# Second half's mixer paced over 331 instead of 277 expert loads, seams tile by tile, first loads ahead of head 1

## The chip, the cores and the metric

The kernel runs on one core of one Trainium2 chip. The metric is the device time of one execution in microseconds: 2576.68 as the median of three runs (2569.09 to 2582.97).

## The reference

512 tokens of width 1024 in float32 pass two blocks. The first: `x = x + concat(deltanet(h), pool(h)) @ w_out` with `h = rmsnorm(x)`, where the mixer is a chunked gated delta rule over 4 heads (short convolution, silu, normed q and k, the inverse of a triangular matrix by chunk, a state carried from chunk to chunk) beside a multi-scale pooling; then an expert layer:

```
q = (xb @ w_query).reshape(t, 8, 2, 128);  scores = einsum("thpc,hpkc->thpk", q, sub_keys)
s1, i1 = top_k(scores[:, :, 0], 16);  s2, i2 = top_k(scores[:, :, 1], 16)
top_s, top_pos = top_k((s1[..., :, None] + s2[..., None, :]).reshape(t, 8, 256), 16)
u = expert_down[idx];  v = expert_up[idx];  act = gelu(einsum("td,thkd->thk", xb, u))
x = x + einsum("thk,thkd->td", softmax(top_s) * act, v)
```

and a final norm. So each token reads 8 x 16 rows of `expert_down` and as many of `expert_up`, 537 MB in all. The second block: `x = x + gate_m * rmsnorm(attention(modulate(rmsnorm(x))))` with a stick-breaking attention of 16 heads, then the same frame around a SwiGLU FFN of inner width 2816. Shifts, scales and gates come from `silu(c) @ ada_w + ada_b`.

## The kernel before

Tokens lie as four tiles (T = 4) of 128. Each engine has its own program; semaphores order them. There are three parts.

**Front.** The first mixer and the query scores run in two halves (h = 0, 1) of 256 tokens. `front_plan(h)` writes the work of a half as a list of stages: `n0`, `tr0` norm and transposes; `p` 0 to 11 projections with convolutions `cv`; `ui`, `gr`, `mk`, `kt`, `ka`, `at`, `kk`, `aa` prepare a chunk of 128; levels 1 to 6 of `v`, `w`, `r`, `u` build the inverse of a chunk; `s1` to `s3` update the state; `pz`, `pl`, `pm` pooling and gate; `wo` output projection; `n1`, `tr1` the norm before the experts; `q` 0 to 15 query units, each followed by its scores `sc`; `gp`, `gs` the gates of the second block. Every engine walks through the same list and does its own share of each stage.

**Loads.** `paced` turns the list into load numbers: each stage's third value, `after`, is the number of expert loads (gathers) that pass before it. All up to the first half's q 6 stands at -1, ahead of the first load; q 7 stands at load 2, and the last stage (`gs` 3) at load 277. A load n is: GpSimd gathers 128 rows of 8 KB (`load`, L1508 to 1518) into a ring of RING = 8 buffers; VectorE multiplies with the tile's tokens and sums (L1816); ScalarE takes the gelu (`weigh`, L1306) and scales a diagonal (L1310); TensorE adds the pair of loads n - 1, n into two banks (`sums`), which frees two ring buffers. 16 loads make one head of one tile, 128 a tile, 512 in all. At a tile's end (loads 124 to 127 and so on) `spread_rows` and `fill_rows` spread the next tile's tokens and `evacuate` writes the tile's sum to x. A head's selection (`select`, `decode`, `spread_head`, `permute`, `place`) runs on VectorE, GpSimd, TensorE two heads ahead. On GpSimd the whole of the -1 part, with the selections of heads 0 and 1 (`sel` 0, `sel` 1), precedes the first eight loads. `Pace.upto(n)` runs the stages due by load n, behind load n's own work in each engine's loop. SP issues weight units (0.52 MB each, eight buffers, three for query units) in the order of the stages, each when the unit before it in its buffer is used, and between them pairs of modulation weights for loads 6 to 123.

Positions (first to last load of a group of stages) before: q 7 to q 15 of the first half 2 to 18; `n0`, `tr0` 19 to 22; `p` 25 to 57; preparation of chunk 2 65 to 77; its levels 77 to 101; state 101 to 107; preparation of chunk 3 108 to 120; its levels 120 to 144; state and pooling 144 to 167; `wo` 172 to 186; `n1`, `tr1` 189 to 192; q 0 to q 15 193 to 224; gates 228 to 277.

**Second block.** After load 511: `act_stats`, `rstd` norm all four tiles (final norm of block one, then the first norm of block two), `pe_transposes` (L670) transposes x, `evac_y` (L1355) modulates into y_hT, and VectorE's `split_hT` splits it in a high and a low part (L1842, L1844) for products of three matmuls each. Weights are split likewise (`split` on ScalarE, GpSimd L1538). GpSimd also fills the zeros of qz (L1543, L1544) behind the second unit. Behind the attention, `branch` takes the norm of the four sums at once and adds (L1882, L1883), then the same norm, transposes and splitting again, the FFN, and `branch` and one store of 2 MB.

## Time and profile before

| | us |
|---|---|
| median of three runs | 2576.68 (2569.09 to 2582.97) |
| profiled execution, its own time | 2573.54 |
| its span | 2571.7 |
| TensorE matmul busy | 1975.4 (77%) |
| VectorE busy | 1311.2 (51%) |
| ScalarE busy | 859.8 (33%) |
| GpSimd busy | 959.4 (37%) |
| first expert load issued, last landed | 255.6, 1801.3 |
| gathers' share of 16 DMA engines | 51.7% of the span |

The span is what the instructions cover; the execution's own time lies 1.8 us above. Busy shares are averages over stages with different limits, so the table by stretch is the one to read: a stretch there runs from the start of one load's dot product to that of another (loads 2, 18, 25, 58; 77, 101; 120, 144; 193, 228, 256; 278, 384, 392 in order of the rows). GB/s is what the DMA moved. In the timeline a row is one instruction or a merged run of like ones; the bracket is the idle time ahead of it and what ended it.

### The profile page before, as it was taken

The page shows a single profiled execution, that of the slowest core. Times are in us where ns is not written, and L with a number is a line of the kernel's source. Part 1 is how long each engine was busy: PE and PEld are TensorE (multiplying, and loading weights), DVE is VectorE, ACT ScalarE, POOL GpSimd, SP SyncE. Part 2 cuts the span into 40 slices and gives each one's busy share as a digit, 9 for nine tenths or more (in the row PEclk, how much of TensorE's full clock was granted, in tenths as well). Part 3 has the DMA queues.
Part 4 walks back from the last instruction along what each step waited for, and adds up shares of the span by engine and source line. Part 5 has one row for each costly group of instructions (what it writes and reads, how often), then busy time and mean ns, then how long its engine had stood idle before and what let it go on. Part 6 is the DMA issues. An engine that isn't in the chain of part 4 may idle for free.

```text
span 2571.7 us, 24837 instructions
## 1 busy us (share of the span) xinstructions
PE 1975.4 (77%) x8704; PEld 1153.5 (45%) x8704; DVE 1311.2 (51%) x2810; ACT 859.8 (33%) x2260; POOL 959.4 (37%) x725
## 2 busy tenths in 40 slices
PE   8897778878788868765556565555698996999996
PEld 7765555435334235311001110000487665888785
DVE  4523547677775554565667666765401542333301
ACT  3112233334343333333333333332423653222212
POOL 1200323356553333444454445544342002444342
PEclk9999888879799889888776787877799998999998
DMA  6112979989989899999999999999021001222221
GB/s 240 36 58 74 405 290 361 383 330 411 392 334 386 331 373 355 375 417 419 420 420 418 420 379 420 420 420 403 33 99 66 1 1 66 98 92 92 78 99 49
DMA packets 100668, 672.54 MB, mean 262 GB/s; under 512 B 11328, under 2 KB 11328, under 8 KB 31552
## 3 DMA queue, kind: packets, MB, share of 16 engines
q0 software_dynamic: 73728, 536.90, 51.7%
q1 hardware_dynamic: 26816, 134.06, 13.6%
q8 instruction: 69, 1.13, 0.2%
q14 instruction: 55, 0.45, 0.0%
HBM read 668.82 MB, written 2.10 MB: 261 GB/s over the span
## 4 chain that ended last, share of the span: by engine, by line
PE 56%; DMA 19%; DVE 8%; issue 6%; ACT 6%; POOL 5%; SPq 0%; DVEq 0%; POOLq 0%; ACTq 0%; PEldq 0%
PE ps L695 55%; DMA arena<-in_experts,arena_u 16%; POOL arena L1515 4%; DVE arena L1816 3%; DMA gtrow<-in_w_ada 1%; ACT arena L1310 1%; DMA arena<-in_w_ada 1%; ACT sel L1306 1%; ACT L1163 1%; PE ps L706 0%; DMA arena<-in_prow 0%; ACT arena L1169 0%; ACT arena L660 0%; ACT L1306 0%; DVE arena L1882 0%
## 5 line engine op out<-in xcount | busy, mean ns | idle before, releaser
L695 PE MATMUL ps<-arena 128*32 128x512 f32 (+4 forms) x4376 | 1125.3, 553 | 377.1 <-ACT arena L1310 362.7
L695 PEld LDWEIGHTS ps<-arena 128*128 128x128 f32 (+1 forms) x4376 | 493.1, 163 | 949.4 <-ACT arena L1310 539.8
L1515 POOL DMA_INDIRECT arena<-in_experts,arena_u x512 | 599.4, 1171 | 846.7 <-PE ps L695 757.5
L1816 DVE CUSTOM_DVE_ANT_0 arena<-arena 128x1024 f32<-128x1024 f32 x512 | 649.3, 1273 | 386.2 <-DMA arena<-in_experts,arena_u 374.6
L695 PE MATMUL ps<-r_low 128*128 128x512 f32 x1824 | 419.5, 392 | 9.7 <-DVE r_low L1844 7.6
L1538 POOL TENSOR_TENSOR r_low<-middle,r_low 128x1024 fp32r<-128x1024 f32 x98 | 235.6, 2404 | 512.7 <-ACT r_low L1349 512.7
L695 PEld LDWEIGHTS ps<-r_low 128*128 128x128 f32 x1824 | 343.3, 189 | 85.3 <-DVE r_low L1844 6.8
L1306 ACT ACTIVATE sel<-sel 128x1 f32<-128x1 f32 x512 | 102.3, 200 | 648.1 <-DVE sel L1816 647.2
L1349 ACT ACTIVATE r_low<-middle 128x1024 fp32r<-128x1024 f32 x98 | 103.6, 1058 | 281.4 <-PE ps L695 281.3
L1310 ACT ACTIVATE arena<-arena,sel 128x32 f32<-128x32 f32 x512 | 164.5, 321 | 17.2 <-ACT sel L1306 0.5
L695 PE MATMUL ps<-arena,consts 128*32 128x32 f32 (+2 forms) x544 | 75.0, 446 | 96.5 <-POOL arena L1498 69.4
L695 PE MATMUL ps<-r_low,r_high 128*128 128x512 f32 x528 | 122.4, 395 | 4.6 <-DVE r_high L1896 4.6
L1299 ACT ACTIVATE arena<-consts,arena 128x32 f32<-128x32 f32 x512 | 120.5, 306 | 0.0
L695 PEld LDWEIGHTS ps<-r_low,r_high 128*128 128x128 f32 x528 | 100.8, 191 | 26.2 <-DVE r_high L1896 5.0
L1894 DVE TENSOR_TENSOR middle<-middle,ps 128x512 f32<-128x512 f32 x22 | 15.1, 688 | 152.6 <-ACT middle L1432 152.6
L695 PEld LDWEIGHTS ps<-arena,consts 128*32 128x32 f32 (+1 forms) x544 | 20.1, 123 | 159.4 <-POOL arena L1498 93.3
L1879 DVE RECIPROCAL stat<-stat 128x4 f32<-128x4 f32 x2 | 0.4, 178 | 176.5 <-ACT stat L1422 176.5
L1491 POOL TENSOR_TENSOR sel<-sel 128x512 f32<-128x512 f32 x32 | 41.8, 1305 | 125.6 <-DVE sel L1614 125.0
L695 PEld LDWEIGHTS ps<-ccol,gtrow 128*128 128x128 f32 x512 | 68.5, 215 | 31.4 <-issue 31.2
L695 PE MATMUL ps<-ccol,gtrow 128*128 128x1 f32 x512 | 70.1, 267 | 7.8 <-DMA gtrow<-in_w_ada 7.8
L1273 ACT ACTIVATE arena<-ps 128x256 f32<-128x256 f32 x32 | 12.3, 384 | 146.8 <-PE ps L695 146.8
L1896 DVE TENSOR_TENSOR r_high<-middle,r_high 128x512 fp32r<-128x512 f32 x22 | 60.8, 2766 | 0.8
(201 smaller groups left out, 1518.9 us busy)
## 6 DMA issues: line engine op xcount, KB each, us to landing
middle<-in_w_late SPq DMA_DIRECT2D x24, 2048.0 KB, 7.4
arena<-in_w_front SPq DMA_DIRECT2D x88, 512.0 KB, 7.7
gtrow<-in_w_ada SPq DMA_DIRECT2D x32, 512.0 KB, 8.3
arena<-in_experts,arena_u POOLq DMA_INDIRECT x512, 12.1
arena<-in_w_ada SPq DMA_DIRECT2D x16, 512.0 KB, 9.0
x<-in_x SPq DMA_DIRECT2D x4, 512.0 KB, 9.0
arena<-in_sub_keys SPq DMA_DIRECT2D x2, 1024.0 KB, 10.4
arena<-in_rows SPq DMA_DIRECT2D x4, 512.0 KB, 10.3
```

The source lines that it names most:

```text
L695: return nc.tensor.matmul(out_, lhsT, rhs, start=start, stop=stop_, skip_group_check=skip)
L1163: nc.scalar.activation(sexp, tops, ACT.Exp, bias=nmax, accum_out=ssum).then_inc(s["sexp"], 1)
L1299: nc.scalar.activation(gated[:, m % 2, 32 * j:32 * j + 32], fold, ACT.Copy, scale=gq[:, i % 4, 4 * q + j:4 * q + j + 1]).then_inc(s["gated ...
L1306: own.step(nc.scalar.activation(gel[:, n % 8:n % 8 + 1], dots[:, n % 8:n % 8 + 1], ACT.Gelu))
L1310: nc.scalar.activation(diag[:, m % 4, 32 * j:32 * j + 32], gated[:, m % 2, 32 * j:32 * j + 32], ACT.Copy, scale=gel[:, n % 8:n % 8 + 1]).t ...
L1349: nc.scalar.activation(u_hi[u % 2], raw_unit(u), ACT.Copy).then_inc(s["u_hi"], 1)
L1491: tt(onehot, onehot, fidx.rearrange("p s (o a) -> p s o a", o=1).broadcast_to([P, 2, 16, 16]), ALU.mult).then_inc(s["fpk"], 1)
L1515: nc.gpsimd.indirect_dma_start(ring[n % RING], None, a["experts"], bass.IndirectOffsetOnAxis(ap=idxq[:, i % 4, k:k + 1], axis=0),).then_in ...
L1538: nc.gpsimd.tensor_tensor(u_lo[u % 2], raw_unit(u), u_hi[u % 2], ALU.subtract).then_inc(s["u_lo"], 1)
L1816: nc.vector.tensor_tensor_reduce(r[:, 0:D], r[:, 0:D], xrep[k % 4], 1.0, 0.0, ALU.mult, ALU.add, dots[:, n % 8:n % 8 + 1]).then_inc(s["dot ...
L1894: own.step(tt(ff[:, j % 2, :], ff[:, j % 2, :], ps[:, 2 * j % 8 + 1, :], ALU.mult))
L1896: tt(act_lo[:, j, :], ff[:, j % 2, :], act_hi[:, j, :], ALU.subtract).then_inc(s["ffd"], 1)
```

## The change

Pace: the second half's projections of odd number take 3 loads instead of 2, its inversion levels 5 instead of 4, its query units 2 to 15 take 4 instead of 2, the first half's query units 8 to 15 take 3 instead of 2. By the same list the positions are then: first half's q 7 to q 15 2 to 26; `n0`, `tr0` 27 to 30; `p` 33 to 71; levels of chunk 2 91 to 121, of chunk 3 140 to 170; `wo` 198 to 212; q 0 to q 15 219 to 278; gates 282 to 331.

First loads: on GpSimd the eight first gathers are issued right behind `sel` 0.

Seams: the norms of tiles 0, 1, 2 are done among the loads, at loads 337, 353, 433 (`beside`; two sums of squares on ScalarE 0 and 4 loads on, scaling and a diagonal matrix of the reciprocal root on VectorE 3 and 7 on, products with that diagonal on TensorE and the modulation on ScalarE 8 on), tile 3 behind the last load. Transposes are now products x with the diagonal. High parts of the activations move from VectorE to ScalarE. At the other two seams the norm goes tile by tile, and the store is four stores of 512 KB.

```diff
@@ -96,7 +96,7 @@
-        add("p", u, 2 if u else 3)
+        add("p", u, 3 if u == 0 or h == 1 and u % 2 == 1 else 2)
...
@@ -154,7 +154,7 @@
-                add("u", (c, lv), 2)
+                add("u", (c, lv), 2 + h)
...
@@ -215,7 +215,7 @@
-        add("q", j, 2)
+        add("q", j, 4 if h == 1 else 3 if j > 7 else 2)
...
@@ -461,6 +461,11 @@
+        def beside(n, lag):
+            gates = STAGES[-1][0]
+            return {gates + 6 + lag: 0, gates + 22 + lag: 1, gates + 102 + lag: 2}.get(n)
...
@@ -510,11 +515,11 @@
-        junk = region(130, D)
+        junk = region(140, D)
+        tdiag = region3(160, T, P)
-        xs2 = region3(144, T, D)
...
@@ -646,35 +651,18 @@
-            sp.wait_ge(s["fin"], T)
-            sp.dma_start(out.rearrange("b (t p) d -> p (b t) d", p=P), x[:, :, :]).then_inc(s["out"], 16)
-            sp.wait_ge(s["out"], 16)
-        def act_stats(eng, k, ready, junk_of):
-                ready(t)
-                if T * k + t > 0:
-                    eng.wait_ge(s["ssq"], T * k + t)
-                nc.scalar.activation(junk_of(t), x[:, t, :], ACT.Square,
-                                     accum_out=stat[:, 0, t:t + 1]).then_inc(s["ssq"], 1)
-            eng.wait_ge(s["ssq"], T * (k + 1))
-            nc.scalar.activation(stat[:, 1, :], stat[:, 0, :], ACT.Sqrt, bias=EPS, scale=1.0 / D).then_inc(s["sd"], 1)
-        def pe_transposes(eng, k, src):
-            for t in range(T):
-                eng.wait_ge(s["xs"], T * k + t + 1)
-                for kd in range(KD):
-                    ins = nc.tensor.transpose(ps[:, kd, t * P:(t + 1) * P], src[:, t, kd * P:(kd + 1) * P], ident)
-                ins.then_inc(s["tr"], 1)
+                sp.wait_ge(s["fin"], t + 1)
+                sp.dma_start(out.rearrange("b (t p) d -> p (b t) d", p=P)[:, t, :], x[:, t, :]).then_inc(s["out"], 16)
+            sp.wait_ge(s["out"], 16 * T)
-        tail_sq = region(8, D)
+        tail_sq, tail_sq2 = region(8, D), region(12, D)
...
@@ -1005,6 +993,17 @@
+            def tile_transposes(t):
+                pe.wait_ge(s["xs"], t + 1)
+                if t == 0:
+                    pe.wait_ge(s["gates_out"], N_GATE)
+                else:
+                    pe.wait_ge(s["a_y"], KD * t)
+                for kd in range(KD):
+                    ins = mm(ps[:, 1 + kd // 4, kd % 4 * P:(kd % 4 + 1) * P], x[:, t, kd * P:(kd + 1) * P], tdiag[:, t, :])
+                ins.then_inc(s["tr"], 1)
...
@@ -1310,6 +1316,27 @@
+            def tile_stats(t, n):
+                if n == 0:
+                    sc.wait_ge(s["acc_out"], t + 1)
+                else:
+                    sc.wait_ge(s["seln"], t + 1)
+                if t + n > 0:
+                    sc.wait_ge(s["ssq"], 2 * t + n)
+                if t == 0 and n == 0:
+                    sc.wait_ge(s["xrep"], 24)
+                nc.scalar.activation(junk, x[:, t, :], ACT.Square, accum_out=stat[:, 0, t:t + 1]).then_inc(s["ssq"], 1)
+                sc.wait_ge(s["ssq"], 2 * t + n + 1)
+                nc.scalar.activation(stat[:, 1, t:t + 1], stat[:, 0, t:t + 1], ACT.Sqrt, bias=EPS, scale=1.0 / D).then_inc(s["sd"], 1)
+            def tile_modulate(t):
+                sc.wait_ge(s["tr"], t + 1)
+                for kd in range(KD):
+                    nc.scalar.activation(y_hT[:, kd, t * P:(t + 1) * P], ps[:, 1 + kd // 4, kd % 4 * P:(kd % 4 + 1) * P], ACT.Identity,
+                                         bias=modc[:, 0, kd:kd + 1], scale=stat_mod(0, kd)).then_inc(s["a_y"], 1)
...
@@ -1330,13 +1357,16 @@
+                if beside(n, 0) is not None:
+                    tile_stats(beside(n, 0), 0)
+                if beside(n, 4) is not None:
+                    tile_stats(beside(n, 4), 1)
+                if beside(n, 8) is not None:
+                    tile_modulate(beside(n, 8))
-            sc.wait_ge(s["acc_out"], T)
-            act_stats(sc, 0, lambda t: None, lambda t: junk)
-            act_stats(sc, 1, lambda t: sc.wait_ge(s["seln"], t + 1), lambda t: junk)
+            tile_stats(T - 1, 0)
...
@@ -1348,16 +1378,18 @@
-            def evac_y(k):
-                sc.wait_ge(s["tr"], T * (k + 1))
-                for kd in range(KD):
-                    nc.scalar.activation(y_hT[:, kd, :], ps[:, kd, :], ACT.Identity, bias=modc[:, 2 * k, kd:kd + 1],
-                                         scale=stat_mod(k, kd)).then_inc(s["a_y"], 1)
+            def high(k, kd):
+                sc.wait_ge(s["a_y"], KD * T + kd + 1 if k == 1 else KD * T)
+                nc.scalar.activation(a_hi[:, kd, :], y_hT[:, kd, :], ACT.Copy).then_inc(s["a_hi"], 1)
+            sc.wait_ge(s["slot_done"], LOADS)
+            tile_stats(T - 1, 1)
-            evac_y(0)
+            tile_modulate(T - 1)
+            for kd in range(KD):
+                high(0, kd)
...
@@ -1410,20 +1442,33 @@
-            def branch(k):
-                for t in range(T):
-                    sc.wait_ge(s["y"], T * k + t + 1)
-                    if k + t > 0:
-                        sc.wait_ge(s["ysq"], (T + 1) * k + t)
-                    nc.scalar.activation(tail_sq, ps[:, 2 * t:2 * t + 2, :].rearrange("p b n -> p (b n)"), ACT.Square,
-                                         accum_out=stat[:, 2, t:t + 1]).then_inc(s["ysq"], 1)
-                sc.wait_ge(s["ysq"], (T + 1) * k + T)
-                nc.scalar.activation(stat[:, 3, :], stat[:, 2, :], ACT.Sqrt, bias=EPS, scale=1.0 / D).then_inc(s["ysq"], 1)
-            branch(0)
-            act_stats(sc, 2, lambda t: sc.wait_ge(s["yfree"], t + 1), lambda t: tail_sq)
-            evac_y(1)
+            def branch(k, t):
+                sc.wait_ge(s["y"], T * k + t + 1)
+                if k + t > 0:
+                    sc.wait_ge(s["ysq"], 2 * (T * k + t))
+                nc.scalar.activation(tail_sq, ps[:, 2 * t:2 * t + 2, :].rearrange("p b n -> p (b n)"), ACT.Square,
+                                     accum_out=stat[:, 2, t:t + 1]).then_inc(s["ysq"], 1)
+                sc.wait_ge(s["ysq"], 2 * (T * k + t) + 1)
+                nc.scalar.activation(stat[:, 3, t:t + 1], stat[:, 2, t:t + 1], ACT.Sqrt, bias=EPS, scale=1.0 / D).then_inc(s["ysq"], 1)
+            def stats_after(t):
+                sc.wait_ge(s["yfree"], t + 1)
+                sc.wait_ge(s["ssq"], 2 * T + t)
+                nc.scalar.activation(tail_sq2, x[:, t, :], ACT.Square, accum_out=stat[:, 0, t:t + 1]).then_inc(s["ssq"], 1)
+                sc.wait_ge(s["ssq"], 2 * T + t + 1)
+                nc.scalar.activation(stat[:, 1, t:t + 1], stat[:, 0, t:t + 1], ACT.Sqrt, bias=EPS, scale=1.0 / D).then_inc(s["sd"], 1)
+            for t in range(T + 1):
+                if t < T:
+                    branch(0, t)
+                if t >= 1:
+                    stats_after(t - 1)
+            sc.wait_ge(s["tr"], 2 * T)
+            for kd in range(KD):
+                nc.scalar.activation(y_hT[:, kd, :], ps[:, kd, :], ACT.Identity, bias=modc[:, 2, kd:kd + 1],
+                                     scale=stat_mod(1, kd)).then_inc(s["a_y"], 1)
+                high(1, kd)
...
@@ -1502,9 +1548,9 @@
-            front = Pace(front_program())
-            front.upto(-1)
+                    if stage == "sel" and arg == 0:
+                        for n in range(RING):
+                            load(n)
...
@@ -1517,8 +1563,9 @@
-            for n in range(RING):
-                load(n)
+            front = Pace(front_program())
+            front.upto(-1)
...
@@ -1805,6 +1852,18 @@
+            def tile_norm(t, n):
+                ve.wait_ge(s["sd"], 2 * t + n + 1)
+                own.step(nc.vector.reciprocal(stat[:, 1, t:t + 1], stat[:, 1, t:t + 1]))
+                if n == 0:
+                    ve.wait_ge(s["pfin"], 16)
+                    ve.wait_ge(s["acc_out"], t + 1)
+                    stt(x[:, t, :], x[:, t, :], stat[:, 1, t:t + 1], prow_fin, ALU.mult, ALU.mult).then_inc(s["seln"], 1)
+                else:
+                    ts(tdiag[:, t, :], ident, stat[:, 1, t:t + 1], None, ALU.mult).then_inc(s["xs"], 1)
...
@@ -1824,22 +1883,17 @@
-            rstd(0)
-            ve.wait_ge(s["acc_out"], T)
-            ve.wait_ge(s["pfin"], 16)
-            for t in range(T):
-                stt(x[:, t, :], x[:, t, :], stat[:, 1, t:t + 1], prow_fin, ALU.mult, ALU.mult).then_inc(s["seln"], 1)
-            rstd(1)
-            ve.wait_ge(s["seln"], T)
-            for t in range(T):
-                ts(xs2[:, t, :], x[:, t, :], stat[:, 1, t:t + 1], None, ALU.mult).then_inc(s["xs"], 1)
+                    if beside(n, 3) is not None:
+                        tile_norm(beside(n, 3), 0)
+                    if beside(n, 7) is not None:
+                        tile_norm(beside(n, 7), 1)
+            tile_norm(T - 1, 0)
+            tile_norm(T - 1, 1)
-                    ve.wait_ge(s["a_y"], KD * k + kd + 1)
-                    nc.vector.tensor_copy(a_hi[:, kd, :], y_hT[:, kd, :]).then_inc(s["a_hi"], 1)
...
@@ -1874,28 +1928,31 @@
-            def branch(k):
-                ve.wait_ge(s["ysq"], (T + 1) * (k + 1))
-                own.step(nc.vector.reciprocal(stat[:, 3, :], stat[:, 3, :]))
-                for t in range(T):
-                    y = ps[:, 2 * t:2 * t + 2, :].rearrange("p b n -> p (b n)")
-                    own.step(stt(tail[:, t % 2, :], y, stat[:, 3, t:t + 1], gtrow[:, k, :], ALU.mult, ALU.mult))
-                    tt(x[:, t, :], x[:, t, :], tail[:, t % 2, :], ALU.add).then_inc(s["yfree" if k == 0 else "fin"], 1)
-            ve.wait_ge(s["y"], T)
-            branch(0)
-            rstd(2)
-            ve.wait_ge(s["yfree"], T)
-            for t in range(T):
-                ts(xs2[:, t, :], x[:, t, :], stat[:, 1, t:t + 1], None, ALU.mult).then_inc(s["xs"], 1)
+            def branch(k, t):
+                ve.wait_ge(s["ysq"], 2 * (T * k + t + 1))
+                own.step(nc.vector.reciprocal(stat[:, 3, t:t + 1], stat[:, 3, t:t + 1]))
+                y = ps[:, 2 * t:2 * t + 2, :].rearrange("p b n -> p (b n)")
+                own.step(stt(tail[:, t % 2, :], y, stat[:, 3, t:t + 1], gtrow[:, k, :], ALU.mult, ALU.mult))
+                tt(x[:, t, :], x[:, t, :], tail[:, t % 2, :], ALU.add).then_inc(s["yfree" if k == 0 else "fin"], 1)
+            def norm_after(t):
+                ve.wait_ge(s["sd"], 2 * T + t + 1)
+                own.step(nc.vector.reciprocal(stat[:, 1, t:t + 1], stat[:, 1, t:t + 1]))
+                ts(tdiag[:, t, :], ident, stat[:, 1, t:t + 1], None, ALU.mult).then_inc(s["xs"], 1)
+            for t in range(T + 1):
+                if t < T:
+                    branch(0, t)
+                if t >= 1:
+                    norm_after(t - 1)
-            ve.wait_ge(s["y"], 2 * T)
-            branch(1)
+            for t in range(T):
+                branch(1, t)
...
```

## Rows read from the trace of the kernel before

**Rows 1.** The page: DMA share in tenths, 40 equal slices of the span.
```profile
DMA  6112979989989899999999999999021001222221
```

**Rows 2.** Busy time by stretch: us, PE, PEld, DVE, ACT, POOL busy (x instructions), clock, DMA share, GB/s.
```profile
267.30:318.60 51.30, 44.38 (x232) 30.91 (x228) 27.27 (x68) 15.52 (x54) 15.01 (x13) 0.97 1.01 410
318.60:367.00 48.40, 33.05 (x148) 20.50 (x150) 16.88 (x47) 16.68 (x52) 9.81 (x11) 0.78 0.77 289
367.00:483.10 116.10, 107.25 (x531) 68.34 (x528) 85.58 (x230) 41.17 (x131) 41.68 (x37) 0.87 0.91 355
554.90:623.50 68.60, 54.72 (x332) 31.07 (x328) 55.06 (x120) 23.86 (x88) 47.85 (x36) 0.93 1.00 409
681.60:754.80 73.20, 64.54 (x356) 32.40 (x356) 50.93 (x106) 31.02 (x96) 37.63 (x30) 0.87 0.84 322
929.00:1044.50 115.50, 95.97 (x430) 59.67 (x432) 60.63 (x157) 36.97 (x132) 37.58 (x33) 0.96 0.91 343
1044.50:1134.70 90.20, 61.76 (x250) 19.09 (x246) 50.68 (x119) 31.16 (x105) 39.58 (x36) 0.87 1.00 405
1201.60:1478.70 277.10, 150.75 (x490) 26.21 (x492) 184.94 (x448) 98.98 (x343) 133.58 (x118) 0.74 1.01 419
1478.70:1500.20 21.50, 14.42 (x86) 3.89 (x84) 16.08 (x49) 10.36 (x36) 9.26 (x9) 0.98 0.83 308
```

**Rows 3.** Timeline, 239 to 263: start, us, engine, line, operation, count, [idle before <-releaser].
```profile
240.07 0.17 DVE L1631 COPY arena<-ps 128x16 f32<-128x16 f32 x1
...
252.54 1.26 POOL L1491 TENSOR_TENSOR sel<-sel 128x512 f32<-128x512 f32 x1 [16.25 <-DVE sel L1614]
...
255.61 1.11 POOL L1515 DMA_INDIRECT arena<-in_experts,arena_u  x1 [0.17 <-issue]
...
255.92 0.17 DVE L1631 COPY arena<-ps 128x16 f32<-128x16 f32 x1
...
257.02 0.94 POOL L1515 DMA_INDIRECT arena<-in_experts,arena_u  x1 [0.30 <-issue]
...
261.40 1.23 DVE L1816 CUSTOM_DVE_ANT_0 arena<-arena 128x1024 f32<-128x1024 f32 x1 [5.31 <-DMA arena<-in_experts,arena_u]
```

**Rows 4.** Timeline, 1798 to 1843, from the last gathers to the attention block.
```profile
1798.22 1.91 PE L695 MATMUL ps<-arena 128*32 128x512 f32 x8 [1.59 <-ACT arena L1310]
...
1803.19 3.54 PE L695 MATMUL ps<-arena 128*32 128x512 f32 x8 [3.06 <-ACT arena L1310]
...
1812.55 1.28 ACT L663 ACT_TABLE_LOAD   x1
1813.84 0.20 ACT L663 ACTIVATE stat<-stat 128x4 f32<-128x4 f32 x1
...
1829.09 5.47 ACT L1355 ACTIVATE upper<-ps,modc 128x512 f32<-128x512 f32 x8 [6.47 <-PE ps L670]
...
1841.78 0.69 DVE L1844 TENSOR_TENSOR r_low<-upper,r_low 128x512 fp32r<-128x512 f32 x1
```

**Rows 5.** Timeline, 2155 to 2190, from the attention block to the FFN.
```profile
2155.82 1.01 ACT L1419 ACTIVATE arena<-ps 128x1024 f32<-128x1024 f32 x1
...
2174.84 5.50 PE L670 MATMUL ps<-consts,arena 128*128 128x128 f32 x32 [20.02 <-DVE arena L1890]
...
2189.09 0.69 DVE L1844 TENSOR_TENSOR r_low<-upper,r_low 128x512 fp32r<-128x512 f32 x1
```

**Rows 6.** Timeline, 2547 to 2572, the end.
```profile
2547.71 1.03 ACT L1419 ACTIVATE arena<-ps 128x1024 f32<-128x1024 f32 x1 [5.74 <-PE ps L695]
...
2554.83 1.28 DVE L1882 SCALAR_TENSOR_TENSOR arena<-ps,stat,gtrow 128x1024 f32<-128x1024 f32 x1
2556.15 1.23 DVE L1883 TENSOR_TENSOR x<-x,arena 128x1024 f32<-128x1024 f32 x1
...
2564.77 0.40 SPq L650 DMA_DIRECT2D out_dram<-x  x1
```

**Rows 7.** DMA issues: tile, queue, kind, count, KB each, median us to landing.
```profile
middle<-in_w_late SPq DMA_DIRECT2D x1, 1024.0 KB, 5.0
```

16 lines of the change are left out of this document (12 added, 4 removed).

## The prediction

> **What bounds the kernel now.** The page's slices come first [rows 1]: one slice is 64.3 us, and the 16 DMA engines stand at 8 or 9 tenths in nearly every one from 257 to 1801 us. In that stretch the 512 gathers of expert rows run, beside the mixer of the second half of the tokens. A gather is 128 rows of 8 KB, 1.05 MB; at the 419 GB/s of the stretch with nothing else in it, 1201.6 to 1478.7 [rows 2], that is 2.50 us each. The second view is the table by stage [rows 2]. Where its rate is near 419, the gathers set the time, and compute beside them is free; where it is lower, compute or a chain of waits sets it, and the lost time is length x (1 - rate/420). So: 1.2 us lost in the first half's last query units (267 to 319), 18.0 in the second half's projections (367 to 483), 1.8 in the inversion of chunk 2 (555 to 624), 17.1 in chunk 3's (682 to 755), 21.2 in the second half's query units (929 to 1044), 5.7 at the tile switch at load 384 (1479 to 1500). The third view is the timeline at four seams where TensorE stands still: the first gathers [rows 3], the hand-over from gathers to the attention block [rows 4], the hand-over to the FFN [rows 5] and the end [rows 6].
>
> **Pacing, 54 more loads.** By the list of stages the last stage moves from load 277 to 331: 8 loads more at the first half's query units 8 to 15, 6 at the projections, 6 + 6 at the levels of chunks 2 and 3, 28 at the second half's query units. No work goes; 54 of the loads that ran alone now run beside compute. A load taken out of the plain stretch saves 2.50 us there, and costs 2.50 where the DMA is already full, nothing but its own sum on TensorE where it isn't (a pair of sums 1.91 or 3.54 us [rows 4], 0.95 to 1.77 a load).
> Query units of the second half: 16 units in 115.5 us, 7.2 a unit with its two loads, of which TensorE is busy 96.0/16 = 6.0 and waits 1.2 [rows 2]. The DMA needs two gathers and a 0.52 MB unit, 5.00 + 1.25 = 6.25. With four loads: DMA 11.25, TensorE 6.0 + 1.9 + 2 x 1.2 = 10.3. The DMA becomes the bound and the 21.2 us go but for about 3: -18.
> Projections: 6 more loads at 1.4 us for the sum (between 0.95 and 1.77, as the clock there is 0.87) where 2.50 is saved: -6 of the 18.0.
> Inversion of chunk 2: only 1.8 lost before: -1. Chunk 3: its levels move from loads 120 to 144 to loads 140 to 170, so the tile switch at loads 124 to 128 falls out of them. A switch alone costs 5.7 and a chunk's inversion alone 1.8, so 17.1 - 7.5 = 9.6 is what their meeting costs; the switch now meets chunk 2's state update instead, and I count half of the 9.6: -5. The next switch, loads 252 to 256, leaves the gate sums (where the stretch 1044 to 1135 ran near full rate) and meets query units: +3. First half's query units: DMA full, 0.
> Sum: -18 - 6 - 1 - 5 + 3 = -27. Bounds: 0 where TensorE fills the added room, -45 if the meeting of switch and levels goes wholly and the projections recover half. Units are fetched three ahead on SP's queue at query units and eight ahead before; a wait for one (the issue follows the use of the unit three back) gets longer in loads, not shorter, so it hides. SP's pairs of modulation weights keep their loads (6 to 123) and their three- to four-load lead; 0, at worst some microseconds.
>
> **First loads ahead of head 1.** GpSimd issues the first eight gathers after head 1's decode; the indices of head 0 stand at 240.1, the first issue is at 255.6 and the first dot product starts at 261.4 [rows 3]. After the edit they are issued from 240.3 on; eight issues, 1.4 us apart at most like the first two, end by 251.5, before head 1's decode starts at 252.5, so nothing on GpSimd queues behind them. VectorE is done with head 1's placing at 256.1 and finds data: 5.3 us earlier. Nothing more is won, as the ring of eight refills only when sums are done; the gathers share the DMA with the ten query units of that time, which may cost TensorE a little: -5, between -10 and 0.
>
> **Seam to the attention block.** Before: last sums begin 1803.19 and take 3.54; an evacuation of 1.0, as long as a square of its size [rows 6], follows at 1806.8; then norms of four tiles twice, a table load, 32 transposes, eight modulations of 0.68, and the last low part at 1841.78 + 0.69 = 1842.5 [rows 4]. Tiles 0 to 2 are now done among the loads, and only tile 3 is left: evacuated 1807.8; square 1.25 (1.03 [rows 6] and the read of its sum), table load 1.28, root 0.2: 1810.6; reciprocal and scaling 1.5 (1.28 [rows 6] and hand-overs): 1812.1; square and root 1.5: 1813.6; reciprocal and the diagonal 0.5: 1814.1; eight products, priced as the 32 transposes at 0.17 each [rows 5] up to twice that: 1815.8; eight modulations of 128 columns, at no more than half of 0.68: 1818.3; then eight pairs of high part (ScalarE, about 0.6) and low part (VectorE, 0.69), the second hiding the first but once: 1819 + 5.6 = 1824.6. That is 17.9 earlier; with the products at the lower clock 16. I take -17. What is late next: GpSimd's two fills of the attention's zeros start when the second low part of the weights is done, now about 1817, and take 7.5, so they end at 1825, as late as TensorE needs them: no slack is left there.
> The pieces for tiles 0 to 2 among the loads: ScalarE waits up to 4 us at loads 337, 353 and 433 (square, root, two table loads) and again four loads later, and 4.4 to 9 us eight loads later, where it stands behind TensorE's products (queued behind it: the next weighing, and so the sums and the refill). The plain stretch bears that: at the tile switch TensorE and ScalarE are taken up for some 14 us and the DMA loses 5.7, so there are about 8 us of slack in the ring. +2; bounds 0 and 3 x (4 + 4 + 9) = 51.
> The row shows the root starting 1.29 us after its table load began, 1.28 of it the load [rows 4]. The Trainium skill (ScalarE: Activation LUTs, What ACT_TABLE_LOAD costs) puts 1.38 us of draining on top of the load; by it the twelve switches added among the loads would take some 17 us more of ScalarE, and the sum would be up to 17 higher; the trace doesn't bear it out.
>
> **Seam to the FFN.** Before, the squares start 2155.8 and the last low part ends 2189.8 [rows 5]. Tile by tile, ScalarE and VectorE alternate: VectorE has four times (0.18 + 1.28 + 1.23 + 0.5 + hand-overs, about 3.4), from 2158.7, so its last diagonal is at 2172.9 against 2174.8 for the old first product; but products of the first tiles wait for all four sums, 32 of them end at 2177.8 instead of 2180.3, and then ScalarE does modulation and high part in turn, 0.68 + 0.6, 10.2 in all, where VectorE made the high parts at about 1.06 a step. Last low part 2188.7: -1, between -4 and +3.
>
> **End.** Before: VectorE starts 2554.83, ends 2564.7, the store of 2 MB is issued at 2564.77 and the span ends at 2571.7 [rows 6]. Now the first tile's sum is squared from 2547.71, its root is there at 2550.5; four times 2.75 on VectorE: 2561.6; the last store is 512 KB. The 2 MB took 6.9 to the end, 1 MB of weights land in 5.0 [rows 7], 1.9 a MB, so a quarter takes about 4.1: 2565.7. -6, between -8 and -4.
>
> **Sum.** -27 - 5 - 17 + 2 - 1 - 6 = -54, from the profiled execution's 2573.5 (span 2571.7 and 1.8 around it): 2519.5. The median of the three runs is 3.1 higher, the lowest 4.4 lower; I give 2520.
>
> **Rivals.**
> A, the clock eats the pacing. Where TensorE stands behind gathers the rows show a granted clock of 0.74 (1201.6 to 1478.7), a mix of 1.2 and 2.4 GHz, and a pair of sums at 3.54 instead of 1.91. The stretched stages come to look like that. If query units run at 1.2 GHz throughout, a period is twice the 7.9 of work and 2.4 of waiting, 18.2, instead of 7.2 + 5.0 = 12.2 for the same loads now. Each such period costs 6.0 and forgoes 18/14 = 1.3, so with four of the fourteen (7.3 x 3.7 = 27) nothing is won by pacing: 2520 + 27 = 2547, chance 0.13. For it: 0.78 and 15 of 48 us lost at 319 to 367 [rows 2]. Against it: the projections hold 0.87 at a DMA share of 0.91 [rows 2], and a TensorE that works at the low clock waits less, after which it has risen again in them.
> The Trainium skill (TensorE: Matmul & The Clock Gate, HAM oscillation) says that a TensorE which waits on DMA between bursts falls back to the low clock at each of them; by it this rival would be the likely case, and this case's sums at 3.54 behind gathers agree with it.
> B, the same further on, slower than before: all fourteen query periods at 18.2 add 14 x 6.0 = 84 to the old time, the seams and the start give back 27: 2573.5 + 84 - 27 = 2630. It decides from 54/7.3, seven and a half of the fourteen. Chance 0.04.
> C, the norm pieces are not hidden: +49 over my +2 at worst, about half of it likely: 2520 + 25 = 2545. For it: ScalarE stands behind TensorE behind VectorE three times. Against: only three places. Chance 0.08.
> D, more comes back: -45 by pacing and -10 at the start, 23 below mine: 2497. For it: the six stretches named first lose 65 us together and my -27 leaves most of that; against: what is left lies in chains (the tile switch, the projections' convolutions) that a wider pace doesn't shorten. Chance 0.15.
> Mine 0.60, 2508 to 2534 as its own range. The range of 8 in 10: from D's end to A's and C's: 2497 to 2549. 0.5% (13 us) is about what a measurement tells from no change: faster needs under 2564. Mine, D, A and C are faster but for their tails: 0.91; same 0.05; slower 0.04.
>
> **What would show it.** The stretch of the query units now at 400 GB/s or more, over some 165 to 170 us for 63 loads; the dot of load 0 at about 256; from the last sums' end to the last low part 18 us, not 36; no drop of the rate below 400 around loads 337 to 349; the tail after the last product 14 us. Wrong: a rate still near 343 in the query units with a clock under 0.8, or time between loads over 2.6 us around the norm pieces.

## The result, and the profile after

The changed kernel takes 2555.99 us in the median of five runs (2551.34 to 2561.97), the kernel before, on the same chip, 2575.01 (2565.13 to 2582.97): a ratio of 0.9933, with a 95% interval of 0.991 to 0.9956. The forecast was 2520, with a range of 2497 to 2549. The kernel is faster, by a third of what was forecast.

The profiled execution has a span of 2554.2 us, 17.5 less than before, at a mean granted clock of 0.878 (0.879 before). With the marks that the prediction used, those 17.5 are made up so:

| part | before | after | difference | forecast |
|---|---|---|---|---|
| start to the first dot | 261.4 | 259.0 | -2.4 | -5 |
| loads: first dot to the evacuation behind the last sums | 1545.4 | 1550.7 | +5.3 | -27 + 2 |
| seam to the attention block | 35.7 | 19.9 | -15.8 | -17 |
| attention block | 313.3 | 315.8 | +2.5 | 0 |
| seam to the FFN | 34.0 | 35.3 | +1.3 | -1 |
| FFN | 357.9 | 357.1 | -0.9 | 0 |
| end | 24.0 | 16.4 | -7.6 | -6 |

So 30 of the 36 us missed are in one row, the stretch with the loads: +5.3 where -25 was forecast. The busy time by stage shows where. Stretches of the changed kernel; columns as in [rows 2]:

```profile
263.10:344.00 80.90, 65.59 (x312) 41.10 (x313) 43.28 (x110) 21.94 (x83) 24.87 (x23) 0.90 0.93 362
344.00:386.30 42.30, 27.30 (x154) 17.32 (x153) 13.50 (x31) 18.16 (x51) 10.58 (x10) 0.87 0.83 328
386.30:521.10 134.80, 113.28 (x568) 70.92 (x564) 99.99 (x268) 46.08 (x149) 47.88 (x45) 0.85 0.90 357
587.70:674.10 86.40, 74.53 (x402) 42.44 (x398) 66.63 (x149) 31.87 (x110) 53.77 (x43) 0.81 1.00 407
691.80:745.20 53.40, 37.15 (x194) 12.87 (x192) 32.00 (x76) 21.76 (x64) 20.12 (x18) 0.87 0.66 254
745.20:823.90 78.70, 53.13 (x276) 24.02 (x276) 64.72 (x148) 30.72 (x108) 49.78 (x42) 0.89 1.00 404
999.70:1182.70 183.00, 143.20 (x668) 74.06 (x668) 112.05 (x275) 69.47 (x243) 79.71 (x70) 0.94 0.95 380
1333.00:1394.90 61.90, 31.51 (x100) 6.93 (x104) 35.26 (x86) 28.50 (x87) 23.72 (x20) 0.65 1.01 421
1394.90:1407.60 12.70, 5.86 (x34) 1.36 (x28) 7.93 (x24) 6.84 (x19) 7.11 (x7) 0.63 0.82 319
```

In order these are the first half's last query units, the norm and transposes behind them, the projections, the levels of chunk 2, the preparation of chunk 3, its levels, the second half's query units, and two stretches around a norm piece. The last column is the rate. Lost time, length x (1 - rate/420) as in the prediction, is 11.2 us in the first half's query units (1.2 before) but 9.3 in the norm and transposes behind them (15.1 before), so 20.5 for 16.3 in the two together; 20.2 in the projections (18.0), 2.7 in chunk 2's levels (1.8), 3.0 in chunk 3's levels (17.1) but 21.1 in the preparation ahead of them, which had been clean, and 17.4 in the second half's query units (21.2). The loss around the first tile switch did not shrink. It moved to whatever now runs at loads 127 to 140.

The timeline of the changed kernel at four places in the loads, columns as in [rows 3]:

```profile
243.50 1.11 POOL L1561 DMA_INDIRECT arena<-in_experts,arena_u  x1 [4.23 <-DVE arena L1678]
...
252.37 0.94 POOL L1561 DMA_INDIRECT arena<-in_experts,arena_u  x1 [0.30 <-issue]
...
255.56 1.26 POOL L1537 TENSOR_TENSOR sel<-sel 128x512 f32<-128x512 f32 x1 [2.25 <-DVE sel L1661]
...
259.02 1.21 DVE L1875 CUSTOM_DVE_ANT_0 arena<-arena 128x1024 f32<-128x1024 f32 x1
...
707.54 0.94 POOL L1561 DMA_INDIRECT arena<-in_experts,arena_u  x1 [16.04 <-PE ps L683]
708.38 1.12 DVE L1781 SCALAR_TENSOR_TENSOR arena<-arena,gates,ps 128x128 f32<-128x128 f32 x4 [15.37 <-PE ps L683]
...
1384.84 2.90 ACT L1337 ACTIVATE upper<-ps,modc 128x128 f32<-128x128 f32 x8 [5.57 <-PE ps L683]
...
1387.59 0.24 ACT L1312 ACTIVATE sel<-sel 128x1 f32<-128x1 f32 x1
...
1388.20 1.28 ACT L1169 ACT_TABLE_LOAD   x1
...
1389.91 1.28 ACT L1312 ACT_TABLE_LOAD   x1
...
1391.82 4.52 PE L683 MATMUL ps<-arena 128*32 128x512 f32 x16 [7.01 <-ACT arena L1316]
...
1395.73 1.25 POOL L1561 DMA_INDIRECT arena<-in_experts,arena_u  x1 [8.45 <-PE ps L683]
```

At the start the eight issues end at 253.3, ahead of head 1's decode at 255.6, and the first dot begins at 259.0. At 708 is the new meeting: the tile switch occupies TensorE, in turn with ScalarE's copies, ahead of the state update's products; VectorE stands 15.4 us for them (line 1781), its dots stand behind that, and GpSimd, which refills the ring, issues nothing for 16.0 us. At 1385 is a norm piece: ScalarE stands 5.6 us behind TensorE's products, modulates for 2.9, weighs a load, pays two table loads of a decode (1.28 each), and TensorE, 7.0 us idle, gets its next sums; GpSimd issues nothing for 8.5 us. The rate falls to 319 for 12.7 us. Such a drop stands behind each of the three pieces, 3.1 us lost in each in this execution.

The seams and the end in the changed kernel, the timeline again, columns as in [rows 3]:

```profile
1809.69 1.02 ACT L1343 ACTIVATE x<-ps 128x1024 f32<-128x1024 f32 x1 [3.44 <-PE ps L683]
...
1811.91 1.28 ACT L1331 ACT_TABLE_LOAD   x1
1813.21 0.20 ACT L1331 ACTIVATE stat<-stat 128x1 f32<-128x1 f32 x1
...
1817.27 3.78 PE L683 MATMUL ps<-arena,x 128*128 128x128 f32 x16 [7.63 <-DVE arena L1865]
...
1821.09 2.90 ACT L1337 ACTIVATE upper<-ps,modc 128x128 f32<-128x128 f32 x8 [3.80 <-PE ps L683]
1823.39 3.50 POOL L1591 MEMSET arena<- 64x4096 f32 x1
...
1824.68 4.91 DVE L1898 TENSOR_TENSOR r_low<-upper,r_low 128x512 fp32r<-128x512 f32 x8 [7.46 <-ACT r_low L1384]
...
2145.44 1.00 ACT L1450 ACTIVATE arena<-ps 128x1024 f32<-128x1024 f32 x1
...
2159.62 9.58 PE L683 MATMUL ps<-arena,x 128*128 128x128 f32 x64 [15.18 <-DVE x L1936]
...
2169.24 0.78 ACT L1469 ACTIVATE upper<-ps,modc 128x512 f32<-128x512 f32 x1 [8.26 <-PE ps L683]
...
2180.03 0.69 DVE L1898 TENSOR_TENSOR r_low<-upper,r_low 128x512 fp32r<-128x512 f32 x1 [0.64 <-ACT r_low L1384]
...
2537.79 1.03 ACT L1450 ACTIVATE arena<-ps 128x1024 f32<-128x1024 f32 x1 [5.74 <-PE ps L683]
...
2543.22 8.29 SPq L656 DMA_DIRECT2D out_dram<-x  x4
...
2549.93 1.22 DVE L1936 TENSOR_TENSOR x<-x,arena 128x1024 f32<-128x1024 f32 x1
```

They answer to [rows 4 to 6]: one tile's norm instead of four between 1809.7 and 1829.6; the squares at 2145.4 and the last low part's end at 2180.7; four stores between 2543.2 and the end, where one was issued at 2564.77.

### The profile page after: what moved, and what is told of

Read it like the earlier page. It is cut to its first block, busy times and chain, and to the rows that moved or that the text cites. A ratio compares the mean times of both kernels' runs of the same rounds, so it can differ in the third digit from the quotient of the medians.

```text
span 2554.2 us, 25041 instructions
## 1 busy us (share of the span) xinstructions
PE 1977.6 (77%) x8768; PEld 1169.5 (46%) x8768; DVE 1300.8 (51%) x2809; ACT 890.2 (35%) x2327; POOL 955.7 (37%) x725
## 4 chain that ended last, share of the span: by engine, by line
PE 56%; DMA 16%; issue 7%; DVE 7%; POOL 7%; ACT 6%; SPq 0%; POOLq 0%; DVEq 0%; ACTq 0%
PE ps L683 56%; DMA arena<-in_experts,arena_u 13%; POOL arena L1561 6%; DVE arena L1875 3%; DMA gtrow<-in_w_ada 2%; DMA arena<-in_w_ada 1%; ACT arena L1316 1%; ACT sel L1312 1%; ACT L1312 1%; ACT arena L1175 1%; DMA arena<-in_prow 0%; ACT upper L1337 0%; POOL arena L1544 0%; DVE arena L1935 0%; ACT L1169 0%
## 5 line engine op out<-in xcount | busy, mean ns | idle before, releaser
L683 PEld LDWEIGHTS ps<-arena 128*128 128x128 f32 (+1 forms) x4376 | 502.5, 166 | 878.5 <-ACT arena L1316 461.2
L683 PE MATMUL ps<-arena,consts 128*32 128x512 f32 (+2 forms) x544 | 79.0, 474 | 120.4 <-POOL arena L1544 90.7
L1951 DVE TENSOR_TENSOR middle<-middle,ps 128x512 f32<-128x512 f32 x22 | 15.1, 688 | 152.6 <-ACT middle L1477 152.6
L683 PEld LDWEIGHTS ps<-ccol,gtrow 128*128 128x128 f32 x512 | 66.9, 211 | 35.7 <-issue 35.6
## 6 DMA issues: line engine op xcount, KB each, us to landing
arena<-in_experts,arena_u POOLq DMA_INDIRECT x512, 11.9
```

The source lines that it names most:

```text
L683: return nc.tensor.matmul(out_, lhsT, rhs, start=start, stop=stop_, skip_group_check=skip)
L1951: own.step(tt(ff[:, j % 2, :], ff[:, j % 2, :], ps[:, 2 * j % 8 + 1, :], ALU.mult))
```

## The experiments

All ratios are against the kernel before, five rounds each, with the 95% interval; 0.001 is 2.57 us. In every kernel whose pace differs from the changed one, the norm pieces were kept at the loads where the change has them (337, 353, 433 and what follows), so that only the pace differs.

**First set: which part.** The changed kernel with all pace edits undone; with the second half's query units stretched alone; with the first loads behind head 1 again; with the modulation of a norm piece four loads later, so that ScalarE doesn't meet the decode.

```diff
# e1_old_pace
-        add("p", u, 3 if u == 0 or h == 1 and u % 2 == 1 else 2)
+        add("p", u, 2 if u else 3)
-                add("u", (c, lv), 2 + h)
+                add("u", (c, lv), 2)
-        add("q", j, 4 if h == 1 else 3 if j > 7 else 2)
+        add("q", j, 2)
-            gates = STAGES[-1][0]
+            gates = 331
# e2_only_q: as e1_old_pace, but
+        add("q", j, 4 if h == 1 else 2)
# e3_loads_behind
-                    if stage == "sel" and arg == 0:
-                        for n in range(RING):
-                            load(n)
...
+            for n in range(RING):
+                load(n)
# e4_modulate_later
-                if beside(n, 8) is not None:
-                    tile_modulate(beside(n, 8))
+                if beside(n, 12) is not None:
+                    tile_modulate(beside(n, 12))
```

> The changed kernel with the pace of before (last stage at load 277); the norm pieces stay at loads 337, 353, 433, the rest as changed. Theory T (the wider pace brings nothing and costs some microseconds, since the first half's query units no longer keep the gathers full and the tile switches meet worse stages): 0 to 8 us faster than the changed kernel, that is 2548 to 2556 where before is 2575 (ratio 0.9895 to 0.993). Rival U (the pace does bring its 27 us and something else eats them): 20 to 27 us slower than the changed kernel, 2576 to 2583 (ratio 1.000 to 1.003).

> The changed kernel with the second half's query units at 4 loads and every other pace as before. Theory T: the query units themselves give back some 12 to 16 of their 21 us lost, and nothing is lost at the start, so 2538 to 2548 (ratio 0.986 to 0.9895). Rival W (the time won at the query units is lost again right behind, so that their pace is worth nothing): 2550 to 2556, the same as with the old pace throughout.

> The changed kernel with the eight first loads behind the selection of head 1, as before. Theory T (first loads are worth the 2.4 us by which the first dot product comes earlier, at most 6): 2 to 6 us slower than the changed kernel, 2558 to 2562. Rival V (the early loads harm the first query units by their DMA): 0 to 5 us faster, 2551 to 2556.

> The changed kernel with ScalarE's modulation of tiles 0 to 2 four loads later (loads 349, 365, 445 instead of 345, 361, 441), so that it neither stands behind TensorE's products nor meets the softmax of load 346, 362, 442. Theory T (three places lose 3.1 us each, 9.3 in all, by ScalarE standing there): no drop of the rate at loads 352, 368, 446 and 7 to 10 us faster, 2546 to 2549. Rival X (these drops come from the norm pieces as a whole, wherever they stand): under 3 us of difference, drops of the same size elsewhere.

| kernel | median us | ratio |
|---|---|---|
| before | 2576.25 | 1 |
| e1_old_pace | 2547.71 | 0.9883 (0.9859 to 0.9906) |
| e2_only_q | 2523.43 | 0.9807 (0.9784 to 0.9831) |
| e3_loads_behind | 2557.47 | 0.9934 (0.9911 to 0.9956) |
| e4_modulate_later | 2551.09 | 0.9904 (0.988 to 0.9929) |

Everything but the pace is worth 0.0117, 30 us. The whole pace of the change makes that worse, 0.9883 to 0.9933, 13 us lost. The query units alone make it better, 20 us won in this set. So 28 of the 54 loads earn, and the other 26 cost more than those earn. The median of e2_only_q lies 15 us below the range that was expected of it. The stages by rate, e1_old_pace first: chunk 2's state update and the preparation of chunk 3, chunk 3's levels, the query units:

```profile
628.70:675.30 46.60, 31.98 (x166) 15.27 (x166) 32.96 (x75) 17.07 (x52) 27.28 (x22) 0.83 0.98 386
675.30:748.30 73.00, 64.24 (x356) 32.35 (x356) 50.83 (x105) 31.06 (x96) 37.70 (x30) 0.87 0.82 313
922.20:1038.00 115.80, 96.21 (x430) 59.82 (x432) 60.77 (x156) 37.21 (x133) 36.12 (x33) 0.96 0.91 342
```

and e2_only_q, the projections and then the query units:

```profile
354.50:468.80 114.30, 105.15 (x530) 67.39 (x527) 86.68 (x228) 41.23 (x131) 39.98 (x37) 0.90 0.92 361
910.40:1083.70 173.30, 132.58 (x592) 71.51 (x593) 109.47 (x271) 65.12 (x227) 76.04 (x67) 0.93 0.99 402
```

At four loads a unit the query units run at 402 and lose 7.4 us, against 21.5 at two: the mechanism of the forecast, nearly at its size. In the changed kernel, where the second tile switch lies in them, the same units run at 380 and lose 17.4.

By time the first loads ahead of head 1 are worth nothing that these intervals of some 6 us either way can tell (0.9934 without them, 0.9933 with). The start of the first dot in the traces tells more, see below.

The later modulation did what it was made for in the trace: the stretches around the first norm piece of e4_modulate_later show no drop any more.

```profile
1338.50:1398.60 60.10, 29.37 (x108) 6.73 (x106) 36.01 (x86) 27.77 (x82) 26.03 (x22) 0.76 1.01 421
1398.60:1408.70 10.10, 6.16 (x26) 1.14 (x24) 7.93 (x25) 6.77 (x18) 3.29 (x3) 0.67 1.01 420
```

From load 332 to the last one 7.7 us are lost there, 13.5 in the changed kernel. By time it is 7 us, with intervals that overlap (0.988 to 0.9929, 0.991 to 0.9956), and it is tried once more below.

**Second set: which of the other loads.** Each on top of e2_only_q. The last one stretches nothing: it puts 20 loads ahead of the second half's first stage, and so moves everything behind it by 20 against the tile switches, which stay at loads 124 to 128 and 252 to 256. Two theories stood here: that the shift costs, above all where the first switch meets the state update, and that a shift as such costs nothing and the stretched stages do.

```diff
# f5_q_and_q0
-        add("q", j, 4 if h == 1 else 2)
+        add("q", j, 4 if h == 1 else 3 if j > 7 else 2)
# f6_q_and_p
-        add("p", u, 2 if u else 3)
+        add("p", u, 3 if u == 0 or h == 1 and u % 2 == 1 else 2)
# f7_q_and_levels
-                add("u", (c, lv), 2)
+                add("u", (c, lv), 2 + h)
# f8_q_shift20
-    add("n0")
+    add("n0", 0, 20 if h == 1 else 0)
```

> The kernel with the second half's query units at 4 loads and all else at the old pace (2523 us), plus the 3 loads at the first half's query units 8 to 15; it moves everything behind by 8 loads, chunk 3's preparation to loads 115 to 128. Theory P (it is the place: a tile switch, loads 124 to 128, that meets the preparation of a chunk costs 15 us or more over the levels' share): +8 to +20, 2531 to 2543. Rival Q (it is the pace itself: each stretched stage costs by its own extra loads, here the first query units): +6 to +8, with chunk 3's preparation and levels together as before (17 us lost).

> The same 2523 us kernel plus the 3 loads at odd projections, which moves what follows by 6 loads (chunk 3's preparation to 113 to 126). Theory P: +5 to +15 and the loss in preparation and levels of chunk 3 above 17 us; the projections stay at 16 to 20 us lost, being bound by TensorE. Rival Q: +4 at the projections and nothing behind them. My blind forecast for this edit alone was -6.

> The same 2523 us kernel plus 5 loads at the levels of both chunks; chunk 3's preparation at 113 to 126 again, its levels at 126 to 156. Theory P: +5 to +15, in the preparation of chunk 3. Rival Q: 0 to +3, as the levels of chunk 2 ran with full gathers before. My blind forecast for this edit alone was -6.

> The same 2523 us kernel with no stage stretched but the whole second half 20 loads later (20 plain loads ahead of its first norm), so that chunk 3's preparation stands at loads 127 to 140 and query units at 213 to 272, nearly as in the changed kernel. Theory P: +10 to +22 (some 10 to 15 in preparation and levels of chunk 3, 4 to 7 where the switch at 256 meets the query units): 2533 to 2545. Rival Q: within 3 us of 2523.

| kernel | loads added | median us | ratio |
|---|---|---|---|
| before | | 2569.01 | 1 |
| f5_q_and_q0 | 8 at the first half's query units | 2542.33 | 0.9893 (0.9871 to 0.9915) |
| f6_q_and_p | 6 at projections | 2537.0 | 0.9865 (0.9841 to 0.9888) |
| f7_q_and_levels | 12 at levels | 2533.56 | 0.9842 (0.9826 to 0.9859) |
| f8_q_shift20 | 20 at no work | 2541.91 | 0.9883 (0.9867 to 0.99) |

e2_only_q has been measured at 0.9807 and, again in the fourth set, at 0.9851; the mean, 0.983, is the base here. Against it the eight loads cost 0.0063 (16 us), the six 0.0035 (9 us), the twelve 0.0012 (3 us); the whole set together costs 27 us (0.983 to the changed kernel's 0.9935, the mean of its two measurements). That the three parts add up to 28 shows little: the base is known to 6 us either way, and it enters the sum three times (with 0.9807 as the base the sum is 46, with 0.9851 it is 12). Of the three only the eight loads stand clear of this noise. Nor are they three separate causes: each of these kernels also moves the second half's query units onto the second tile switch, which e2_only_q has just behind them. The pure shift costs 0.0053, 14 us, with no stage stretched, so the theory that a shift as such costs nothing fell. The stages of f8_q_shift20: the preparation of chunk 3, its levels, the query units.

```profile
682.80:740.40 57.60, 42.03 (x218) 15.90 (x214) 32.22 (x74) 21.71 (x64) 20.91 (x20) 0.85 0.65 251
740.40:804.30 63.90, 44.19 (x244) 21.12 (x244) 53.55 (x119) 26.93 (x92) 45.12 (x35) 0.88 0.97 386
979.40:1160.30 180.90, 139.92 (x674) 73.99 (x676) 109.07 (x273) 72.21 (x247) 79.87 (x70) 0.94 0.96 385
```

The first two lose 23.2 + 5.2 = 28 us where e1_old_pace loses 3.8 + 18.6 = 22 in its two stages, and 15 in the query units where e2_only_q loses 7.4. Around the first switch and around the second more is lost by this view.

**Third set: which meeting.** The later modulation on top of e2_only_q; a milder spread of the query loads, with output projections of the mixer stretched instead; a shift by 28, past the state update; and the query units stretched in the kernel before.

```diff
# g1_q_modulate_later: as e2_only_q, with the edit of e4_modulate_later
# g2_wo3_q3: as g1_q_modulate_later, but
-        add("wo", k, 2)
+        add("wo", k, 2 + h)
-        add("q", j, 4 if h == 1 else 2)
+        add("q", j, 3 if h == 1 else 2)
# g3_q_shift28: as e2_only_q, but
-    add("n0")
+    add("n0", 0, 28 if h == 1 else 0)
# g4_before_q4: the kernel before, but
-        add("q", j, 2)
+        add("q", j, 4 if h == 1 else 2)
```

> The best so far (only the second half's query units at 4 loads, ratio 0.981) with the modulation of tiles 0 to 2 four loads later. If the two effects add: 4 to 6 us less, ratio 0.978 to 0.980 (about 2519 where before is 2573). If the later modulation was worth only what it moved by chance: 0.981 again.

> As the kernel with the modulation later, but the second half's output projection at 3 loads a unit (8 loads more, from loads 172 to 195) and its query units at 3 (201 to 247), so that the switch at 252 to 256 still meets the gate sums. Theory: the output projection ran at 7.7 us lost with TensorE 98% busy, and 8 more loads give back 4 to 6 of them; query units at 3 loads need 8.75 us of DMA and 8.8 of TensorE and lose 3 to 6 more than at 4. Sum 0 to -3 us against the best, ratio 0.977 to 0.980. Rival: the query units at 3 stay bound by TensorE and the sum is +5, ratio 0.982.

> As the kernel with the second half 20 loads later (ratio 0.988), but 28 later: the tile switch at loads 124 to 128 now meets the last levels of chunk 2 (105 to 129) and not its state update (129 to 135, before 121 to 127). Theory S (it is the state update, for which VectorE stood 15.4 us before the next dot product, that makes the switch dear): preparation and levels of chunk 3 lose under 15 us together instead of 28, and the levels of chunk 2 some 5 to 10; ratio 0.983 to 0.986, more where the query units, now 221 to 277, meet the second switch. Rival R (any meeting of switch and compute costs the same): 0.988 again.

> The kernel before with nothing but the second half's query units at 4 loads. If the query pace is worth the same without the seams: 20 to 26 us faster, ratio 0.990 to 0.992; my blind forecast for it was -18, 0.993. If it needs the other edits: 0.997 or above.

| kernel | median us | ratio |
|---|---|---|
| before | 2571.72 | 1 |
| g1_q_modulate_later | 2525.05 | 0.9822 (0.9791 to 0.9852) |
| g2_wo3_q3 | 2536.33 | 0.9888 (0.9863 to 0.9912) |
| g3_q_shift28 | 2539.25 | 0.9887 (0.9863 to 0.991) |
| g4_before_q4 | 2557.61 | 0.9946 (0.9927 to 0.9966) |

The shift by 28 costs as much as that by 20 (0.9887, 0.9883), so the state update is not special, and that theory fell: from chunk 2's levels to the end of chunk 3's the trace loses 28.7 us with the shift by 20 and 29.5 with that by 28. The query units alone in the kernel before are worth 0.0054, 14 us, less than the 20 to 26 that were expected of them beside the first ratio of e2_only_q. The milder spread is worse by time, 17 us against g1_q_modulate_later. In the trace three loads a unit leave 13.5 us lost in the query units and four leave 7.4, which is 6 of the 17; where the rest is was not found. The later modulation adds nothing to e2_only_q that the interval tells.

**Fourth set: which switch.** Twenty loads put in behind the first switch, so that only the second one lands elsewhere (in the query units, as in the change); the shift at n0 with the old pace; and both main kernels again, for the spread between sets.

```diff
# h1_q_shift_at_n1: as e2_only_q, but
-    add("n1", 0, 1)
+    add("n1", 0, 21 if h == 1 else 1)
# h2_old_pace_shift20: as e1_old_pace, but
-    add("n0")
+    add("n0", 0, 20 if h == 1 else 0)
# h3_only_q_again: e2_only_q
# h4_changed_again: the changed kernel
```

> The kernel with only the query units at 4 loads (ratio 0.981), with 20 plain loads ahead of the second half's norm before the experts: nothing of the mixer moves, the query units go to loads 213 to 272 and meet the tile switch at 252 to 256. If the second switch is dear there: 6 to 10 us lost more in the query units, ratio 0.983 to 0.985. If it is only the first switch that costs: 0.981.

> The changed kernel with the old pace throughout (ratio 0.988), the second half 20 loads later: the first switch meets state update and preparation of chunk 3, the second (252 to 256) meets the gates as before. If the first switch is dear there: 10 to 14 us slower than the old pace in place, ratio 0.992 to 0.994. If only the second switch costs: 0.988.

> The kernel with only the query units at 4 loads, a second time: 0.981 (0.978 to 0.984), if its first ratio was no lucky one; anything above 0.984 takes part of the 20 to 24 us between it and the old pace back.

> The changed kernel a second time, in one job with the others: 0.991 to 0.996 of before.

| kernel | median us | ratio |
|---|---|---|
| before | 2571.24 | 1 |
| h1_q_shift_at_n1 | 2533.65 | 0.9851 (0.9826 to 0.9875) |
| h2_old_pace_shift20 | 2552.12 | 0.9922 (0.9896 to 0.9949) |
| h3_only_q_again | 2532.76 | 0.9851 (0.9826 to 0.9877) |
| h4_changed_again | 2556.25 | 0.9937 (0.9915 to 0.9958) |

By time the second switch in the query units costs nothing against h3_only_q_again (0.9851 with it and without) and 5 us against the mean of the base. h3_only_q_again itself came out above the 0.984 that was to show whether the first ratio was a lucky one: in part it was. The profile of h1_q_shift_at_n1 shows its mark, 15 us lost in the query units, where that of h3_only_q_again shows 8.3. First h1_q_shift_at_n1 (chunk 3's levels, query units), then h3_only_q_again (query units):

```profile
674.30:747.20 72.90, 64.65 (x358) 32.51 (x360) 49.19 (x106) 31.46 (x99) 37.31 (x30) 0.87 0.83 316
972.50:1152.50 180.00, 139.73 (x668) 74.19 (x668) 109.87 (x274) 71.06 (x243) 74.95 (x70) 0.94 0.96 385
```

```profile
921.00:1095.90 174.90, 134.80 (x604) 71.56 (x604) 110.77 (x270) 66.20 (x231) 72.82 (x67) 0.93 0.98 400
```

The spans of the two profiled executions differ by 10.4 us as well (2540.7 and 2530.3), but the medians of six by 0.9, and the interval leaves room for some 6 us either way. The other traces side with the profile. Of the kernels with four loads a unit, the ten executions with the second switch among these units lose 12.7 to 21.6 us in them, the four without (e2_only_q, h3_only_q_again, g1_q_modulate_later, g4_before_q4) 7.4 to 8.3. With the old pace the shift at n0 costs 0.0039, 10 us (the intervals, 0.9896 to 0.9949 and 0.9859 to 0.9906, overlap a little). So a shift ahead of the first switch costs 14, 15 and 10 us in three kernels, in the first two of which the second switch meets other work too, and one behind it 0 to 5 in one.

## Why the prediction was wrong, step by step

**Seams, start, end, norm pieces: right as a sum.** Forecast -5 - 17 + 2 - 1 - 6 = -27, measured -30 by time (e1_old_pace, some 6 us either way). In the trace the seam to the attention block gives 15.8 of the 17 (the products took 3.78 us where at most 2.7 was allowed, the modulations 2.90 of 2.5 allowed), the end 7.6 of the 6 (the stores of the first tiles go under the sums of the next, and the span ends 3.0 us after the last addition), and the seam to the FFN +1.3 for -1, inside its bounds. There the 32 products took 9.58 us, priced at 4.9: the price was that of 32 transposes, one record each, and a product has two.

The step "First loads" gave 2.4 of its 5 us in this execution: the issues came 12.1 us earlier, but VectorE is done with the placing of head 1's indices, behind which the dot stands, only as the dot starts at 259.0; it was done at 256.1 before [rows 3]. This start moves from one execution to the next. In the 15 profiled executions with the early issue the first dot begins between 251.9 and 259.5, in the mean at 256.3, as the forecast had it; in the three without (before, g4_before_q4, e3_loads_behind) at 260.5 in the mean. So the traces bear out 4.2 of the 5.

The norm pieces cost 9.3 us in this trace for the +2 of the forecast, 4.7 in the second execution of the changed kernel (h4_changed_again), 5 to 8 in e1_old_pace and the two of e2_only_q, and nothing at the same loads in the two kernels that lack them. The step counted each of ScalarE's waits alone against 8 us of slack; the wait, the modulation and the decode's two table loads come one behind the other, and there the slack is gone. Rival C is thus true at a part of its 25. By time this is not resolved: 7 us in e4_modulate_later, 2 in g1_q_modulate_later.

On those table loads the Trainium skill (ScalarE: Activation LUTs, What ACT_TABLE_LOAD costs) gives a draining beside the load itself. The root at 1813.21 starts 1.30 us after its load began, 1.28 of it the load: the trace disagrees, as it did before the change.

**Query units: right.** Forecast -18 for the stage, measured -14 in the kernel before (g4_before_q4), and -14 from e1_old_pace to the mean of the two measurements of e2_only_q. The loss falls from 21.5 to 7.4 where 3 was expected to be left. In the changed kernel itself the sign that was named, 400 GB/s or more over 165 to 170 us, did not come: it is 380 over 183. Rivals A and B, the clock, did not come: the granted clock in the stretched units is 0.94 in the changed kernel and 0.93 in e2_only_q, between the levels of 1.2 and 2.4 GHz but close to the upper, though TensorE is now idle 40 of 183 us. The Trainium skill (TensorE: Matmul & The Clock Gate, HAM oscillation) describes a TensorE that waits on DMA between short bursts and starts each of them at the lower clock. The trace doesn't show that in these units; the plain stretch, at 0.65 in the row of 1333 us, comes nearer to it.

**The step that failed is "Pacing", in its other 26 loads.** It gave them -6 (projections), -1 (chunk 2), -5 (chunk 3), +3 (second switch) and 0 (the first half's query units): -9. Measured, together: +27. The parts by time are +9, +3 for both chunks, 0 to +5 and +16, none of them free of the others (see the second set). The mistake behind all of them was to price a load by the work of the stage that receives it, and to hold the rest of the schedule for unmoved. Where the 27 us lie, two profiled executions of each kernel show better. Lost time by stage, us, by the same formula; the stages run between the dots of loads 2, 33, 72, 91, 170, 219, 282 and 511 in the changed kernel, 2, 25, 58, 77, 144, 193, 256 and 511 in e2_only_q:

| stage | changed kernel, h4_changed_again | e2_only_q, h3_only_q_again | difference | forecast |
|---|---|---|---|---|
| first half's query units to its transposes | 20.5, 20.1 | 18.8, 21.5 | 0 | 0 |
| projections | 20.2, 20.6 | 16.1, 16.1 | +4 | -6 |
| from there to chunk 2's preparation | 11.9, 11.3 | 12.8, 12.4 | -1 | 0 |
| chunk 2's levels to chunk 3's | 27.0, 28.0 | 17.1, 22.8 | +8 | -1 - 5 |
| state, pooling, output projection, norm | 21.3, 23.7 | 19.1, 14.1 | +6 | 0 |
| second half's query units | 17.4, 18.3 | 7.4, 8.3 | +10 | +3 |
| gates and plain stretch | 14.8, 14.8 | 13.0, 16.3 | 0 | 0 |
| sum | 133, 137 | 104, 112 | +27 | -9 |

Two executions of one kernel differ by up to 6 us in a row of this table, so its small differences say nothing.

First, the shift. Each added load moves all later stages against what is tied to load numbers, the tile switches among it. The step said that the switch leaves chunk 3's levels and "now meets chunk 2's state update instead, and I count half of the 9.6": a gain of 5. The levels did become clean (17.1 lost before, 3.0 after), but the new meeting loses 21.1 where nothing was lost, 24 for 17 in all. With a shift alone and no stage stretched (f8_q_shift20, g3_q_shift28, h2_old_pace_shift20), 28.5 to 29.5 us are lost from chunk 2's levels to chunk 3's, where the eight executions without a shift ahead of them lose 17.1 to 23.3; by time such a shift costs 10 to 15 us, about half of the 27. The rows at 708 us show how it works in one place: a chain in which VectorE waits for TensorE and GpSimd for both, 16 us without an issue. The largest single difference, +10 for +3, is in the second half's query units, which the shift puts onto the second switch. Only 4 of these 10 lie around it (loads 244 to 268: 6.7 and 7.4 us lost in the changed kernel, 3.5 and 2.8 in e2_only_q); what the others meet was not found.

The eight loads of the first half show the shift best. They cost 16 us by time, but in the trace of f5_q_and_q0 hardly anything is lost in the stages that got them (21.4 us where the two of e2_only_q lose 18.8 and 21.5). It is lost further on, in stages with no load added: 24.8 in the projections for 16.1, 21.6 in the second half's query units for about 8. Those two stretches of f5_q_and_q0:

```profile
383.00:508.50 125.50, 111.79 (x517) 72.09 (x513) 87.72 (x232) 39.03 (x130) 38.99 (x36) 0.81 0.87 337
946.00:1131.30 185.30, 141.18 (x662) 74.05 (x664) 109.59 (x275) 70.41 (x238) 75.76 (x68) 0.93 0.92 371
```

Second, the chains of a decode and of the modulation weights. What ended TensorE's waits, in the projections of e2_only_q and then of the changed kernel; columns: instruction, what it waited for, us in total, times, longest:

```profile
PE ps L683 <- ACT arena L1316: 3.8, 2, 3.3
PE ps L683 <- POOL arena L1544: 3.7, 1, 3.7
PE ps L683 <- DMA gtrow<-in_w_ada: 1.7, 1, 1.7
```

```profile
PE ps L683 <- ACT arena L1316: 8.8, 2, 5.5
PE ps L683 <- POOL arena L1544: 7.2, 2, 3.8
PE ps L683 <- DMA gtrow<-in_w_ada: 5.3, 2, 4.2
```

The 6 loads were priced at their sums, 1.4 us each. TensorE's busy time did grow by only 6.0 [rows 2 before, 113.28 after]; but the stage grew by 18.7, since TensorE's idle time there went from 8.9 to 21.5. It waits for the weighing, for GpSimd's part of a decode (two such waits now, not one), and for the modulation weights, which the forecast had put at 0. Part of that is the shift again: in f5_q_and_q0, with no load added to the projections, the waits for GpSimd and for the weights are 5.4 and 4.2 us, and TensorE is busy 6.6 us longer too, at a granted clock of 0.81 where e2_only_q has 0.90. The first half's stretched query units of the changed kernel show the same three waits (8.8, 4.0 and 3.9 us; 7.1 for the weighing alone in e2_only_q), but what they lose more, the norm and transposes behind them lose less. So a load brings with it the decode and the weights that are tied to load numbers, and in a stage with TensorE as the bound they stop it. How the 27 us divide between the switches and these chains was not separated.

What also made the step look safe was that the table by stage was taken for a sum of the kernel. Two profiles of one and the same program differ by as much as its smaller terms: in e2_only_q and h3_only_q_again the preparation and levels of chunk 3 lose 17 and 21 us and all stages together 104 and 112, the first dot begins at 251.9 and 259.0, and the medians of the two are 9 us apart.

**The best version** is e2_only_q, the change with only the second half's query units stretched: 0.9807 and 0.9851 (2523.43 and 2532.76 us), by the mean of the two some 27 us below the changed kernel and 44 below the one before. With the later modulation (g1_q_modulate_later, 0.9822) it is the same within the intervals.

## What to carry to other kernels

Where work is paced by a counter and some events are tied to that counter, each added tick moves all later stages against those events; ask first where they will land, and price that beside the stage itself. Stretch the last stage before the plain stretch, where a shift meets nothing more, and only one whose loss is a steady one of its own. To price a tick by the busy time it adds is right for the busy time alone: look in the list of waits for what else arrives with it.

## What the runs showed of the hardware

- TensorE's eight fp32 products of a 128x128 block with the diagonal, two records each, took 3.78 us behind 7.6 us of idleness, 0.24 a record, at a granted clock of 0.50, the lower of its two levels throughout. The 32 products at the next seam, behind 15.2 us of idleness, took 9.58 us, 0.15 a record, at 0.76 over the run.
- How long the gathers' issue stops doesn't alone decide whether the rate falls. In e4_modulate_later this issue came after a stop of 11.8 us, in the stretch that ran at 421 (timeline, columns as in [rows 3]); in the changed kernel one of 8.5 us stands in the stretch at 319. What the ring held at the start of each stop was not read.

```profile
1365.96 1.90 POOL L1561 DMA_INDIRECT arena<-in_experts,arena_u  x1 [11.80 <-PE ps L683]
```
